# A two-layer hybrid decoder trunk: modulation beside the first attention, each tile normalised behind its residual addition, a router with moving tokens, buffers at fixed places

## The reference, cut to what matters

```python
c_act = silu(c)
for layer in range(2):
    mod = c_act @ w_mod[layer] + b_mod[layer]            # (B, 6*1024)
    shift_m, scale_m, gate_m, shift_f, scale_f, gate_f = split(mod, 6)
    h = rms_norm(x, norm_mix[layer]) * (1 + scale_m) + shift_m
    x = x + gate_m * token_mixer(h)      # dilated attention, 8 heads; retention, 4 heads; w_out
    h = rms_norm(x, norm_ffn[layer]) * (1 + scale_f) + shift_f
    f = swiglu(h) if layer == 0 else moe_swiglu(h)       # D_FF 2816; top 2 of 8 experts, 3584
    x = x + gate_f * f
```

## Time and profile before

| | us |
|---|---|
| median of 3 runs | 4616.14 (4613.1 to 4796.35) |
| the profiled execution, its own time | 4578.78 |
| its span on the slowest core | 4577.1 |
| spans of the 8 cores | 4534.5 to 4577.1 |
| TensorE, VectorE, ScalarE, GpSimd busy | 3189.4, 1694.2, 1146.6, 760.9 |
| mean granted TensorE clock | 0.809 of 2.4 GHz |

### The profile page before, as it was taken

The page is one execution under the profiler, slowest core; times in us unless marked ns, Lnnn a source line. Parts: engine busy times, 40 slices in busy tenths (PEclk is TensorE's granted clock), DMA queues, the critical chain, the costliest instruction groups (busy, mean ns, idle before and its releaser), DMA issues.

```text
span 4577.1 us, 59941 instructions; the slowest of 8 cores (4534.5 to 4577.1 us)
## 1 busy us (share of the span) xinstructions
PE 3189.4 (70%) x20346; PEld 1754.7 (38%) x20355; DVE 1694.2 (37%) x2545; ACT 1146.6 (25%) x2003; POOL 760.9 (17%) x668
## 2 busy tenths in 40 slices
PE   3677654556899966677455552669976788889876
PEld 1233343423343422333334222325543545455543
DVE  0488854333133335888544325112111212121211
ACT  2244432313110112444233032111111213021211
POOL 0100011120035460000111300201121111111120
PEclk9676666767899987766666775779998999999998
DMA  5311010013411122100110150897787969595966
GB/s 171 82 14 12 4 17 8 8 19 115 74 28 28 24 72 60 14 9 5 17 13 3 20 205 24 139 148 123 115 140 111 158 90 163 95 161 89 150 97 98
DMA packets 278861, 334.36 MB, mean 73 GB/s; under 512 B 67823, under 2 KB 205167, under 8 KB 278480
## 3 DMA queue, kind: packets, MB, share of 16 engines
q0 software_dynamic: 243696, 254.15, 37.7%
q1 hardware_dynamic: 34788, 75.30, 4.8%
HBM read 505.93 MB, written 36.96 MB: 119 GB/s over the span
## 4 chain that ended last, share of the span: by engine, by line
PE 51%; DVE 14%; DMA 13%; issue 9%; ACT 8%; POOL 3%; another core or an unknown queue 1%; DVEq 1%; ACTq 0%; POOLq 0%; SPq 0%; PEldq 0%
PE ps L1245 12%; PE ps L1273 10%; PE ps L931 7%; DMA s_w2s<-moe_w 4%; PE ps L450 3%; DMA s_ring<-moe_w 3%; POOL s_x L500 3%; PE ps L535 3%; PE ps L585 2%; DVE s_acc L707 2%; PE ps L680 2%; PE ps L657 2%; DVE s_hbf L477 1%; DVE s_acc L691 1%; ACT s_sa L1248 1%
## 5 line engine op out<-in xcount | busy, mean ns | idle before, releaser
L1245 PE MATMUL ps<-s_hgT,s_ring 128*128 128x0 bf16 (+1 forms) x5824 | 849.5, 307 | 228.4 <-DVE s_gT L1249 100.6
L1245 PEld LDWEIGHTS ps<-s_hgT,s_ring 128*128 128x128 bf16 x5824 | 552.9, 101 | 526.1 <-issue 293.2
L1249 DVE TENSOR_TENSOR s_gT<-ps,s_sa 128x384 bf16<-128x384 f32 (+1 forms) x364 | 233.0, 640 | 846.0 <-ACT s_sa L1248 798.9
L1273 PE MATMUL ps<-s_w2s,s_gT 128*128 128x512 bf16 x2072 | 460.0, 386 | 69.3 <-DMA s_w2s<-moe_w 68.9
L1248 ACT ACTIVATE s_sa<-ps 128x384 bf16<-128x384 f32 (+1 forms) x364 | 199.3, 556 | 527.0 <-PE ps L1245 484.2
L1273 PEld LDWEIGHTS ps<-s_w2s,s_gT 128*128 128x128 bf16 x2072 | 204.8, 99 | 321.9 <-issue 86.0
L931 PE MATMUL ps<-s_hT,s_w 128*128 128x512 bf16 x1408 | 307.0, 381 | 21.2 <-DMA s_w<-ffn_w 21.2
L450 PE MATMUL ps<-s_wm,s_cact_rep 128*128 128x512 f32 x384 | 191.7, 657 | 129.8 <-DMA s_wm<-w_mod 128.8
L1248 ACT ACT_TABLE_LOAD x56 | 71.8, 1283 | 755.5 <-PE ps L1245 746.0
L500 POOL TENSOR_TENSOR s_x<-s_x,s_tmpf 128x1024 f32<-128x1024 f32 x96 | 221.8, 2342 | 189.0 <-DVE s_tmpf L495 189.0
L594 DVE RECIPROCAL s_rsb<-s_rsb 128x512 f32<-128x512 f32 x64 | 214.5, 3351 | 91.8 <-ACT s_rsb L592 91.8
(11 more groups left out here) (219 smaller groups left out, 4354.8 us busy)
## 6 DMA issues: line engine op xcount, KB each, us to landing
s_ring<-moe_w POOLq DMA_DIRECT2D x112, 1024.0 KB, 18.5
s_w2s<-moe_w POOLq DMA_DIRECT2D x56, 1024.0 KB, 26.9
s_wm<-w_mod SPq DMA_DIRECT2D x24, 2048.0 KB, 9.4
s_w<-ffn_w POOLq DMA_DIRECT2D x10, 1024.0 KB, 10.8
s_x<-x SPq DMA_DIRECT2D x4, 2048.0 KB, 9.1
out<-s_x SPq DMA_DIRECT2D x4, 2048.0 KB, 7.9
s_wqkv<-w_in POOLq DMA_DIRECT2D x24, 256.0 KB, 4.4
s_w2s<-ffn_w POOLq DMA_DIRECT2D x5, 1024.0 KB, 8.5
```

What stands on the lines that cost most here:

```text
L1245: ins = e.matmul(o, lhsT=ring[s_][:, kc, j * 128:(j + 1) * 128], rhs=r, start=(kc == 0), stop=(kc == 7))
L1249: k.op("dve", lambda e: e.tensor_tensor(out=gT[:, fc, c0:c0 + width], in0=ps[:, bb, 0:width], in1=sa[z][:, 0:width], op=ALU.mult), reads=[ ...
L1273: ins = e.matmul(ps[:, b0 + hf, :], lhsT=gT[:, fc, b * 128:(b + 1) * 128], rhs=w2s[:, fc, hf * 512:(hf + 1) * 512], start=(fc == 0), stop= ...
```

## The change

- **Places.** Buffers are no longer allocated per stage behind a barrier. `place` gives each a fixed offset, and `alias` lets a new buffer inherit the waits of whatever overlapped it. All barriers go but one, at the end of `attention`. x has a buffer per tile in all its uses, hT one per four tiles, ss, sq and rs one per tile.
- **Start.** Only shift and scale of the first sub-layer are computed ahead: four blocks in eight loads (`load_wmi`), each block as eight matmuls of 32 equal columns in four 32-row strips of PSUM (`mod_parts`), summed over the strips by one more matmul (`mod_sum`). x comes behind them in eight loads. The bias table is computed once per head and copied to 128 rows by 24 transfers on SP. Then, for each tile, `stats` and `apply`.
- **Modulation.** The other 20 blocks run as `mod_step`, one before every ninth unit of the first attention (unit 5, 14, 23, 32, 41 of each head pair); the result goes to DRAM (modscr) and is loaded when a sub-layer opens. w_mod comes in pieces of 512 KB in three slots.
- **Normalising.** In both out projections and in the last down of the feed-forward, `apply(t - 2)` is called behind the matmuls and the residual update of tile t.
- **Router.** lo is computed on POOL. The router's columns are the weights and 512 tokens move, for four tiles at once; the 8 x 512 result is turned back by four small matmuls.
- **Feed-forward.** Its first group has two chunks instead of the last; w13 of the first group is loaded ahead of the out projection.
- **Experts.** The first tile's ring and all of its w2 are loaded ahead of the routing arithmetic and of the gather.
- esb and psb of the attention are one buffer; cs and mask2 are loaded at the start of each retention; the out projection's weights are two buffers; its PSUM pairs are three.

```diff
+    def alias(self, b):
+        m = dict(b.w)
...
+        for o in self.all:
+            if o is not b and o.hi > b.lo and b.hi > o.lo:
+                o.dead = True
+                for src in (o.w, o.r):
+                    for key, t in src.items():
+                        if key not in m or m[key].val < t.val:
+                            m[key] = t
+        b.w, b.r = m, {}
...
+    def mod_parts(halves, Bh, bank, first_kc):
+        def mm(e):
+            for q in range(4):
+                kc = first_kc + q
+                ins = e.matmul(ps[32 * q:32 * q + 32, bank, :], lhsT=crep[:, kc, :], rhs=halves[:, q, :], start=(first_kc == 0), stop=(first_kc == 4))
...
+    def mod_sum(mev, Bmev, bm_ap, Bbm, bank, m):
+        def mm(e):
+            e.matmul(ps[0:m, bank, :], lhsT=sel[:, 0:m], rhs=mev, start=True, stop=False)
+            return e.matmul(ps[0:m, bank, :], lhsT=onesf[0:1, 0:m], rhs=bm_ap, start=False, stop=True)
...
+        def stats(self, t):
+            k.op("act", lambda e: e.activation(out=self.junk[:], in_=x[:, t, :], func=AF.Square, accum_out=ss[:, t:t + 1]),
+                 reads=[XT[t]], writes=[self.Bj, Bss[t]])
+            k.op("act", lambda e: e.activation(out=sq[:, t:t + 1], in_=ss[:, t:t + 1], func=AF.Sqrt, bias=float(EPS), scale=1.0 / D),
+                 reads=[Bss[t]], writes=[Bsq[t]])
+
+        def apply(self, t, banks, want=None):
...
+            k.op("dve", lambda e: e.reciprocal(out=rs[:, t:t + 1], in_=sq[:, t:t + 1]), reads=[Bsq[t]], writes=[Brs[t]])
+            k.op("dve", lambda e: e.scalar_tensor_tensor(out=tmp, in0=x[:, t, :], scalar=rs[:, t:t + 1], in1=self.A[:], op0=ALU.mult, op1=ALU.mult),
+                 reads=[XT[t], Brs[t], self.BA], writes=[self.Btmp[s2]])
+            if want is not None:
+                k.op("dve", lambda e: e.tensor_tensor(out=tmp, in0=tmp, in1=self.shift[:], op=ALU.add), reads=[self.Btmp[s2], self.Bs], writes=[self.Btmp[s2]])
+                k.op("act", lambda e: e.copy(out=hbf, in_=tmp), reads=[self.Btmp[s2]], writes=[self.Bhbf[s2]])
+            else:
+                k.op("dve", lambda e: e.tensor_tensor(out=hbf, in0=tmp, in1=self.shift[:], op=ALU.add), reads=[self.Btmp[s2], self.Bs], writes=[self.Bhbf[s2]])
...
+            k.op("act", lambda e: e.copy(out=hT[:, :, t * 128:(t + 1) * 128], in_=psbf(bank).rearrange("p (c n) -> p c n", c=8)),
+                 reads=[PB[bank]], writes=[HT[t // 4]])
...
+        for i_ in range(24):
+            k.dma("sp", bass.AP(ebrep, i_ * 128 * 384, [[384, 128], [1, 384]]), bass.AP(ebscr, i_ * 384, [[0, 128], [1, 384]]),
+                  reads=[ebscr_buf], writes=[ebrep_buf])
...
+    def mod_step(bank):
...
+        for qt in range(4):
+            j = 4 * i + qt
+
+            def mm(e):
+                for q in range(2):
+                    c, kc = (2 * qt + q) % 4, 2 * qt + q
+                    ins = e.matmul(ps[32 * c:32 * c + 32, bank, :], lhsT=crep[:, kc, :], rhs=wm[:, j % 3, q, :], start=(qt < 2), stop=(qt >= 2))
+                return ins
+            k.op("pe", mm, reads=[Bwm[j % 3], B["const"]], writes=[PB[bank]])
+            mod_more()
+        k.op("act", lambda e: e.copy(out=mev[:], in_=ps[:, bank, :]), reads=[PB[bank]], writes=[Bmev])
+        mod_sum(mev[:], Bmev, bm[:], Bbm, bank, 32)
+        k.op("act", lambda e: e.copy(out=mrow[:], in_=ps[0:1, bank, :]), reads=[PB[bank]], writes=[Bmrow])
+        k.dma("sp", bass.AP(modscr, l * 6 * D + nb * 512, [[512, 1], [1, 512]]), mrow[:], reads=[Bmrow], writes=[modscr_buf])
...
+            for ui, u in enumerate(units):
+                if l == 0 and ui % 9 == 5:
+                    mod_step(ui // 9 % 2)
+                scores(u, ui)
...
+        for t in range(NT + 2):
+            if t < NT:
+                b0 = 2 * (t % 3)
...
+                k.op("pe", mm, reads=[BattnT, BretT] + Bwo, writes=[PB[b0], PB[b0 + 1]])
+                residual_update(2 * l, t, (b0, b0 + 1), tmpo[:, t % 2, :], Bt2[t % 2])
+                n2.stats(t)
+            if t >= 2:
+                n2.step(t - 2)
...
+        k.op("pool", lambda e: e.tensor_tensor(out=lo[:, s2, :], in0=tmp, in1=hbf, op=ALU.subtract), reads=[Btmp, Bhbf], writes=[Blo[s2]])
...
+        if t % 4 == 3:
+            router_logits(g)
+
+    def router_logits(g):
...
+                for kc in range(8):
+                    m = hT[:, kc, g * 512:(g + 1) * 512] if lh == 0 else loT[:, g % 2, kc, :]
+                    ins = e.matmul(ps[0:8, 7, :], lhsT=rhl[:, rr, kc, :], rhs=m, start=(n == 0), stop=(n == 23))
...
+        for g in range(3):
+            load13(0, g)
+        for g in range(FG):
+            load2(0, g)
...
+    fgroups = [(0, 2), (2, 4), (6, 4), (10, 4), (14, 4), (18, 4)]
```

More of the change, by code:

```diff
@@ L133, in guard @@
         E.seen = seen
+        if self.spare is None:
+            self.spare = E.h.alloc_register("spare")
+        E.h.reg_mov(self.spare, 0)
     def _deps(self, reads, writes):
         deps = {}
+        for b in list(reads) + list(writes):
+            assert not b.dead, b.name
         def add(t):
@@ L492, in residual_update @@
[L492 to L499 removed]
+    tab, (Btab_,) = P("btab", [33, 8], F32, 60)
@@ new lines, in attention, with vp @@
+            for tb in range(4):
+                def vp(tb=tb):
+                    bk = 4 + (tb % 2)
+                    def mm(e):
+                        for kc in range(8):
+                            ins = e.matmul(ps[:, bk, :], lhsT=wqkv[:, s, kc, 2, :], rhs=hT[:, kc, tb * 512:(tb + 1) * 512],
+                                           start=(kc == 0), stop=(kc == 7))
+                        return ins
+                    k.op("pe", mm, reads=[Bw[s], HT[tb]], writes=[PB[bk]])
+                    k.op("act", lambda e: e.copy(out=vT[:, tb * 512:(tb + 1) * 512], in_=ps[:, bk, :]), reads=[PB[bk]], writes=[BvT])
+                vp_steps.append(vp)
@@ new lines, in attention @@
+            LAG = 2
+            for ui, u in enumerate(units):
+                if l == 0 and ui % 9 == 5:
+                    mod_step(ui // 9 % 2)
+                scores(u, ui)
+                if ui >= LAG:
+                    pv(units[ui - LAG], ui - LAG)
+            if units:
+                for uj in range(max(len(units) - LAG, 0), len(units)):
+                    pv(units[uj], uj)
+            k.op("dve", lambda e: e.reciprocal(out=acc[:, 1, :], in_=acc[:, 1, :]), reads=[Bacc], writes=[Bacc])
@@ new lines, in retention, with mmkv @@
+                    k.op("pe", tr, reads=[Bsrc, B["constp"]], writes=[PB[bank]])
+                    k.op("act", lambda e: e.copy(out=dstT[:, g4 * 512:(g4 + 1) * 512], in_=psbf(bank)[0:64, 0:512]), reads=[PB[bank]], writes=[BdstT])
+            for g4 in range(4):
+                bk = 4 + g4
+                def mmkv(e):
+                    for q4 in range(4):
+                        c = 4 * g4 + q4
+                        ins = e.matmul(ps[0:64, bk, q4 * 128:(q4 + 1) * 128], lhsT=rkd[:, c, :], rhs=rv[:, c, :], start=True, stop=True)
+                    return ins
+                k.op("pe", mmkv, reads=[Brkd, Brv], writes=[PB[bk]])
@@ new lines, in down @@
+                    residual_update(1, t, (b0, b0 + 1), tmpf[:, t % 2, :], Btf[t % 2])
+                    if n2:
+                        n2.stats(t)
+                if n2 and t >= 2:
+                    n2.step(t - 2)
+        load2(0)
+        n = len(fgroups)
+        for gi in range(n):
+            if gi + 1 < n:
+                load13(gi + 1)
+            up(gi)
+            if gi == n - 1:
+                n2 = nxt()
+                n2.load()
+            if gi > 0:
+                down(gi - 1)
+            if gi + 1 < n:
+                load2(gi + 1)
@@ new lines, in moe @@
+        ys = [yss[:, q, :] for q in range(2)]
+        sas, Bsa = Q("sam", [128, 2, 512], BF16, 94208, n=2)
+        sa = [sas[:, q, :] for q in range(2)]
+        for E in k.E.values():
+            k._wait(E, k._deps([Btab], []))
+        why = "the counts and indices are worked out here and lie within their bounds"
+        rows = mybir.ALL_ENGINES
+        cnt = []
+        for i in range(NTILE):
+            cnt.append(nc.values_load(tab[0:1, i, 0:1], engines=rows, min_val=0, max_val=CAP, skip_runtime_bounds_check_because=why))
```

1559 lines of the change are left out of this document (757 added, 802 removed).

## The result

The changed kernel is slower. Its median is 4846.7 us (4801.3 to 4906.5, 4 runs), that of the kernel before in the same comparison 4614.6; the ratio is 1.044, 95% interval 1.034 to 1.055. The forecast was 4747, inside 4555 to 4880.

A forecast was written before the change was run, and what follows sets the result against it. No engine bounds everywhere; stages where engines take turns (1066 us) and attention can move. Terms -54 + 220 + 6 - 8 - 19 - 22 + 38 - 30 = +131 give 4709.9 us profiled, 4747 in runs; range 4555 to 4880.

The forecast's parts named there:

- Steps, +220 forecast: Attention 0: twenty modulation steps among its units add 220 us in all, bounds 140 to 340.
- take 11 net: Attention 0: a modulation step totals 12.7 us, less 1.5 for work ACT and VectorE have left meanwhile.
- Rival 1: Attention 0: modulation hides, a step costs 2 us net, total 4567; decides from 4.5 us a step; chance 0.12.
- Woven stages: Normalisation woven behind tiles: out projection 0 -19 us (-44 to 13), feed-forward to attention 1 -22 (-33 to -4).
- Reciprocal 0.2, multiply 1.28, shift 1.23: Out projection 0: VectorE's normalising operations per tile, in us, part of 5.3 added to a projection of 3.6.
- the forecast's signs: What would show it right, including 9 to 12 us a tile in the first woven stage, TensorE idle behind VectorE.
- 165 of 140 to 197: Out projection 0 to feed-forward: 140 us, or 197 if the clock falls in each gap; 165 taken.
- rival 5: Woven stages: every TensorE burst is cold, 13, -4, 65 us, 77 more, total 4824; chance 0.08.
- rival 2: Woven stages: clock stays at 2.4 GHz, -44, -33, -13 us, 87 less, total 4660; chance 0.18.
- Router stage, +38: Out projection 1 with router: 306 us instead of 268, between 255 and 333 by clock; +38 (-13 to 65).
- Start, -54: Start to first attention: 162 us instead of 216, sixteen tiles of 6.9 us each; -54 (-65 to -40).
- Retention, +6 and -8: Both retentions: rotary table load +6 us (0 to 10), out projection weights without the barrier -8 (-16 to 4).

## Why the prediction was right, and where it wasn't

The sign and the reason for it held: the modulation steps cost more than everything else saved. On core 0 the sum was +131 and came out +209. The run's slowest core adds 14 to that, and the median lies 45 above the profiled run, where the forecast had added 37. (The forecast's sum is 4709.8, not 4709.9; nothing hangs on it.)

- **Steps, +220 forecast, +250 measured.** The step worked out at 12.7 took 12.65 in the one shown and 12.4 in the mean, with the strips overlapping as the earlier trace rows suggested, the fourth pair's wait (2.9 idle) and the copy. The error was "take 11 net": ScalarE and VectorE's leftover work hid nothing. Put ahead of the attention, the same steps cost the same. Rival 1 (2 us a step) was far off for this form of the step; with four places and late sums the net cost is 4.8, beside rival 1's turning point of 4.5.
- **Woven stages: the failed term.** "Reciprocal 0.2, multiply 1.28, shift 1.23" took the multiply from a loop in which GpSimd was idle. Held by GpSimd's addition it takes 3.39. So the 5.3 us from projection to projection became 7.2, which over 14 tiles is 27 us, against the 29 and 26 that out projection 0 and feed-forward missed by; the first woven stage took 12.9 us a tile, where the forecast's signs had 9 to 12, and feed-forward's +4 lies outside its own -33 to -4. How much of the clock's price to take, 165 of 140 to 197, was a choice that no row settles; a burst took 6.28 us, where it takes 3.45 at full clock and would take twice that at half, nearer rival 5 than rival 2.
- **Router stage, +38 and measured +30.** Here two thirds of the low clock's price had been taken. Three tiles of four take 16.7 us, inside the forecast's 13.7 to 17.3, and the fourth, with the logits, 28.5.
- **Start, -54 and measured -42.** The chain of 6.9 us a tile was right (6.76); the first tile came at 67.5 us instead of 52. Its A stands on VectorE behind an operation on a small table (q_gain), whose load SP issues behind x's eight: issued at 42.7, it landed 21.2 us later.
- **Retention, +6 and -8, measured 0.** Removing the barrier bought nothing for the out projection's weights: TensorE waits 18.2 and 20.9 us for them in the two layers, against 19.3 and 18.8 before. Its wait for the retention's own weights grew by 7.8 us, beside the +6. What took as much off elsewhere in these stages is open.
- **Gather, +29 and -59, measured +13 and -50.** The gather did wait for all thirteen loads: the last landed at 3161.8, the gathered tokens at 3163.0. What was wrong is the price of a load: thirteen took 87 us (3074.7 to 3161.8), 6.7 each, not 8.1, so that the first expert matmul came at 89 us and not 105. The down projection's missing wait was worth 9 less than taken. The two errors offset each other to 7, which is luck.

The prediction did not see the size of the choice between weaving and not weaving. It gave -19 and -22 as what the woven stages save. A separate loop in the same places would have saved 77 and 67 (184.4 to 107.3, 636.7 to 569.8), since the modulation had left both. The alternative needed only rows that stood there: 3.6 + 2.5 a tile apart, 8.9 to 12.5 woven.

## What to carry to other kernels

Before weaving a step into a loop, write down each engine's queue for one turn: if tile t's product stands ahead of tile t-2's normalisation on VectorE, and the transposes ahead of the next matmuls on TensorE, the woven loop is a serial chain and costs the sum of its links, here 12.9 us a tile in place of 6.3 for two plain loops. Issue the older tile's work first; that order alone brought 181 us, and the addition's engine 100 more on top of it. A wait placed inside TensorE's queue costs more than itself: removing 2.9 us of wait from a step took 6.7 us off it, since the parts then ran together and what followed ran at a higher clock.

## What the runs showed of the hardware

- **GpSimd holds VectorE.** A GpSimd addition of 128x1024 float32 (2.34 us) makes a VectorE multiply with two SBUF tensors that starts 0.03 us behind it end 1.08 us behind the addition's end: 3.39 us for 1.28. One that starts 0.77 us behind takes 2.66 and also ends 1.08 behind, so VectorE's work is put off to the addition's end and not slowed in proportion. It goes the other way too: with the order alone, a subtraction of GpSimd in the router stage that starts inside such a multiply takes 3.10 us in place of 2.12. A gate product, which has one of its inputs in PSUM, takes its 1.23 us beside the same addition (at 1198.15 in the changed kernel, 0.4 us of it shared). With the addition on VectorE the multiply is 1.28 in all 16 tiles. The Trainium skill (SBUF — State Buffer, "SBUF: two separate sides") says that a VectorE operation with two SBUF inputs and a GpSimd operation that reads SBUF exclude each other for the whole instruction; the trace agrees.
- **Idle matmuls paid for themselves.** 24 matmuls a tile whose result nobody reads raised the granted clock from 0.69 to 0.98 and shortened the mean period from 12.9 to 10.5 us.
- **Float32 matmuls on four strips of 32 columns** run together: with four places the eight of a step take 1.92 to 3.64 us in one go, where one alone takes 1.88 at the lower clock and 1.04 at the full one, so that eight in turn would take 8.3 even there.
- **Loads of one queue land in their order here.** The gather behind thirteen loads of POOL's queue landed 1.2 us after the last of them, and weights asked for behind seven loads landed after those.
- **One stall, more than one price.** The attention's mean clock rose from 0.65 to 0.77 when the steps stopped waiting, and the units between the steps gained with it, 0.906 to 0.866 us in the median.
